# Chunks 16 and 17 of the input projection in three passes, the state norm inside the scan, two products on GpSimd

## The reference

```python
for l in range(DEPTH):                       # DEPTH = 2
    z = rmsnorm(x, norm_mix_g[l]) @ w_in[l]
    z_a, z_b, z_c, z_dz, z_dxbc, z_ddt, z_g = split_cols(z, IN_SPLITS)
    y_a = mixer_spatial_gating(z_a, ...)     # A
    y_b = mixer_pool(z_b, ...)               # B
    y_c = mixer_rwkv7(z_c, ...)              # C: decayed receptances r, keys k, state in 2 chunks of 128
    y_d = mixer_ssd(z_dz, z_dxbc, z_ddt, ...)   # D: ends in rmsnorm(y * silu(z_dz), d_norm_g)
    proj = einsum('btkc,kcd->btkd', stack([y_a, y_b, y_c, y_d]), w_branch[l])
    x = x + (sum(sigmoid(z_g) * proj) @ w_out[l])
    x = x + channel_mixer(rmsnorm(x, norm_ffn_g[l]))
return rmsnorm(x, norm_final_g)
```

## Time and profile before

| | us |
|---|---|
| median of 3 runs (lowest, highest) | 2014.98 (2013.32, 2015.97) |
| the profiled execution, its own time | 2014.89 |
| its span in the trace | 2013.1 |
| PE busy in the span | 1992.4 (99%) |
| PE weight loads | 1651.4 (82%) |
| DVE busy | 1518.5 (75%) |
| ACT busy | 1184.6 (59%) |
| POOL busy | 62.8 (3%) |
| granted TensorE clock, mean | 0.998 of full speed |

### The profile page before, as it was taken

The page is one execution under the profiler, slowest core; times in us unless marked ns, Lnnn a source line. Parts: engine busy times, 40 slices in busy tenths (PEclk is TensorE's granted clock), DMA queues, the critical chain, the costliest instruction groups (busy, mean ns, idle before and its releaser), DMA issues.

```text
span 2013.1 us, 31612 instructions
## 1 busy us (share of the span) xinstructions
PE 1992.4 (99%) x12922; PEld 1651.4 (82%) x12922; DVE 1518.5 (75%) x1498; ACT 1184.6 (59%) x1071; POOL 62.8 (3%) x56
## 2 busy tenths in 40 slices
PE   8999999999999999999999999999999999999998
PEld 8988899999999988999977777777777777777775
DVE  4888537766535779546688888888888888888887
ACT  4654445433334555444477776777767777677775
POOL 0200011000000020011000000000000000000000
PEclk9999999999999999999999999999999999999999
DMA  8523225555554523234469998999989999899994
GB/s 311 178 98 123 85 105 192 182 189 189 184 183 157 189 105 119 92 106 147 155 265 368 363 365 339 358 364 364 365 341 356 368 360 369 341 355 368 360 367 190
DMA packets 70792, 503.96 MB, mean 250 GB/s; under 512 B 8320, under 2 KB 8576, under 8 KB 9984
## 3 DMA queue, kind: packets, MB, share of 16 engines
q1 hardware_dynamic: 69792, 499.03, 66.1%
q10 hardware_dynamic: 864, 2.95, 0.4%
HBM read 500.90 MB, written 1.05 MB: 249 GB/s over the span
## 4 chain that ended last, share of the span: by engine, by line
PE 59%; DVE 2%; ACT 0%; issue 0%; DVEq 0%; ACTq 0%
PE g L536 38%; PE m L536 19%; PE m L1268 1%; DVE ring_low L2235 0%; PE m L831 0%; DVE arena L2145 0%; DVE h L2560 0%; PE m L586 0%; PE g L1030 0%; DVE rstd L2558 0%; DVE mg_low L2271 0%; PE m L1261 0%; DVE arena L2260 0%; DVE rep L2260 0%; DVE arena L2132 0%
## 5 line engine op out<-in xcount | busy, mean ns | idle before, releaser
L2295 DVE TENSOR_TENSOR ring_low<-ring,we_high 128x2048 fp32r<-128x2048 f32 x336 | 765.5, 2289 | 122.2 <-ACT we_high L1671 121.4
L1671 ACT ACTIVATE we_high<-ring 128x2048 fp32r<-128x2048 f32 x334 | 640.9, 1919 | 269.8 <-PE g L536 170.0
L536 PE MATMUL g<-h_high,ring_low 128*128 128x256 f32 x1328 | 372.2, 282 | 0.0
L536 PE MATMUL g<-we_high,hg_high 128*96 128x512 f32 x896 | 355.8, 397 | 0.0
L536 PE MATMUL g<-ring_low,hg_high 128*96 128x512 f32 x896 | 353.0, 394 | 0.0
L536 PE MATMUL g<-we_high,hg_low 128*96 128x512 f32 x896 | 352.0, 393 | 0.0
L536 PEld LDWEIGHTS g<-h_high,ring_low 128*128 128x128 f32 x1328 | 249.4, 189 | 0.0
L536 PE MATMUL g<-h_low,w_high 128*128 128x256 f32 x720 | 200.4, 282 | 0.0
L536 PE MATMUL g<-h_high,w_high 128*128 128x256 f32 x720 | 200.2, 281 | 0.0
L536 PEld LDWEIGHTS g<-we_high,hg_low 128*96 128x96 f32 x896 | 144.3, 161 | 63.3
L536 PEld LDWEIGHTS g<-we_high,hg_high 128*96 128x96 f32 x896 | 144.7, 161 | 58.8
(11 more groups left out here) (340 smaller groups left out, 3193.2 us busy)
## 6 DMA issues: line engine op xcount, KB each, us to landing
ring<-stream SPq DMA_DIRECT2D x472, 1024.0 KB, 4.8
sw<-sw_in SPq DMA_DIRECT2D x1, 1088.0 KB, 10.9
sw<-sw_in ACTq DMA_DIRECT2D x1, 1088.0 KB, 7.1
x<-x_in SPq DMA_DIRECT2D x4, 256.0 KB, 4.3
out<-h ACTq DMA_DIRECT2D x4, 256.0 KB, 2.8
cc<-cc_in SPq DMA_DIRECT2D x1, 816.5 KB, 12.2
rep<-rep_in SPq DMA_DIRECT2D x1, 768.0 KB, 13.5
rep<-rep_in ACTq DMA_DIRECT2D x1, 768.0 KB, 6.8
```

The lines of the kernel that those rows point to most:

```text
L536: return pe.matmul(o, a, b, start=start, stop=stop, skip_group_check=True)
L1671: A(we_high[n % 3][:, :], ring[:, slot, :], ACT.Copy).then_inc(high_ready, 1)
L2295: TT(ring_low[:, slot, :], ring[:, slot, :], we_high[n % 3][:, :], ALU.subtract).then_inc(low_ready, 1)
```

## The change

What is computed stays the same; two chunks are multiplied another way, and work moves between engines and places.

- Chunks 16 and 17 are multiplied in three passes, by two more `scan_high` on ACT and two more `scan_low` on DVE in each layer. A third buffer, `scan_third`, takes the rounded chunks 16 and 18; 17 goes into `scan_even`. The tile `kk` moves to make room, `st` too.
- PE does chunk 18 ahead of the head sums `ss`, and DVE subtracts chunk 18 ahead of `removal` (the scaled keys `kk`).
- DVE's two products for `ar[.., 1, :]` and `ka` go to POOL, which makes the first after ACT's two exponentials and the second after DVE's `k2`. PE waits for both (`ar_ready`) before it turns the keys.
- DVE's scaling of D's output by the norm moves from `mixer_d` into level 1 of half 0 of `mixer_c`; the reciprocal stays.
- `SIDE` gets two more quarters at `cg`, one more before the second pair of scores in each half, and one before `n` of half 1: 70 in all.

```diff
-SCAN_SPLIT = (14, 15, 18)
+SCAN_SPLIT = (14, 15, 16, 17, 18)
-SIDE = [("cg", 4), ("sr", 4), ("kt", 3)]
+SIDE = [("cg", 6), ("sr", 4), ("kt", 3)]
-    SIDE += [(f"s1{_c}", 1), (f"s2{_c}", 1), (f"s3{_c}", 1)]
+    SIDE += [(f"n{_c}", _c), (f"s0{_c}", 1), (f"s1{_c}", 1), (f"s2{_c}", 1), (f"s3{_c}", 1)]
...
+        scan_third = part("scan_third", 23144, [CW])
...
-            return (scan_even if n % 2 == 0 else scan_odd)[:, :]
+            return {14: scan_even, 15: scan_odd, 16: scan_third, 17: scan_even, 18: scan_third}[n][:, :]
...
+                pe.wait_ge(S["ar_ready"], 2 * (l + 1))
                 pe.wait_ge(S["ab_ready"], l + 1)
                 turn(l, "kt", [ka[:, j, 0:P] for j in range(4)])
...
                 mixer_b(l)
+                project(l, 18, NZ)
                 pe.wait_ge(S["krsq"], l + 1)
                 pe.wait_ge(S["by_head_ready"], 1)
                 head_sums(l, "ss", tmp1)
-                project(l, 18, NZ)
...
                 q.step(A(small[:, 63:64], eps, ACT.Exp))
+                act.wait_ge(S["pooled"], l + 1)
+                scan_high(l, 16)
                 act.wait_ge(S["d_endraw"], l + 1)
...
                 drain(l, "st", A(st[:, :, :], mb("st")[:, :].rearrange("p (g n) -> p g n", g=2), ACT.Copy))
+                scan_high(l, 17)
...
+                pool.wait_ge(S["e_ready"], 4 * l + 2)
+                for i in range(2):
+                    g_done(pool, l, ("c", i))
+                G.tensor_tensor(ar[:, :, :, 1, :], zc[:, 0:4, 1:T + 1].rearrange("p j (c t) -> p j c t", c=NCH),
+                                e_in.rearrange("p j (c t) -> p j c t", c=NCH), ALU.mult).then_inc(S["ar_ready"], 1)
+                pool.wait_ge(S["k2_ready"], l + 1)
+                G.tensor_tensor(ka[:, :, :], k2[:, :, :], e_neg[:, :, :], ALU.mult).then_inc(S["ar_ready"], 1)
...
+                    if i == 1:
+                        scan_low(l, 16)
...
                         decay_sum(l)
+                        scan_low(l, 17)
                         mix(l, 4)
...
                 decay_mid(l)
-                removal(l)
                 mixer_a_out(l)
                 scan_low(l, 18)
+                removal(l)
                 mix(l, 5)
...
-                q.add(TT(ar[:, :, :, 1, :], rc, e_in.rearrange("p j (c t) -> p j c t", c=NCH), ALU.mult), v_seq)
-                q.step(TT(ka[:, :, :], k2[:, :, :], e_neg[:, :, :], ALU.mult))
                 q.step(TT(nb[:, :, :], aa[:, :, :], e_neg[:, :, :], ALU.mult), S["ab_ready"])
+                dve.wait_ge(S["ar_ready"], 2 * (l + 1))
...
+                        if (c, lv) == (0, 1):
+                            mixer_d_norm(l)
```

More of the change, by code:

```diff
@@ L265, in trunk @@
         cs = tiles(21648, H, P)
-        st = tiles(22672, 2, T)
+        st = tiles(12840, 2, T)
         seg1 = tiles(25192, H, P)
@@ L290, in trunk @@
         kept = small[:, 128:128 + L * CT].rearrange("p (l j) -> p l j", l=L)
-        w_log, c_sum, aa, kk = (tiles(at, 4) for at in (26216, 27240, 9744, 23144))
+        w_log, c_sum, aa, kk = (tiles(at, 4) for at in (26216, 27240, 9744, 15976))
         e_in, e_neg, e_ex = (tiles(at, 4) for at in (7696, 8720, 22120))
@@ L787, in mixer_c @@
                     half = lambda hd: slice(64 * (hd % 2), 64 * (hd % 2) + 64)
+                    side(f"n{c}")
                     for q in range(2):
@@ L809, in mixer_c @@
                                     fill(l, st_, last)
-                        if p:
-                            side(f"s{p}{c}")
+                        side(f"s{p}{c}")
                     for v in range(LEVELS - 1):
@@ L1515, in mixer_c @@
                 for c in range(NCH):
-                    side(f"s1{c}", f"s3{c}")
+                    side(f"n{c}", f"s3{c}")
                     for v in range(LEVELS):
@@ L1568, in z_highs @@
                     if n < N_SLOTS:
-                        act.wait_ge(chunks_used, chunk0(l) + NZ - (1 if (2 * l * N_LATE + n) % N_SLOTS < 3 else 0))
+                        act.wait_ge(chunks_used, chunk0(l) + NZ - 1)
                     A(half_slot(l, m, b), half_ring(ring, l, m, b), ACT.Copy).then_inc(z_high_ready, 1)
@@ L2006, in mixer_d, with mixer_d_norm @@
                 m_done(dve, l, "dn")
-                q.step(V.reciprocal(rstd[:, :], rms[:, :]))
+                q.step(V.reciprocal(rms[:, :], rms[:, :]))
+            def mixer_d_norm(l):
                 for j in range(4):
-                    ins = V.scalar_tensor_tensor(yD[:, j, :], yD[:, j, :], par(l, "norm_d", j), rstd[:, :], ALU.mult, ALU.mult)
+                    ins = V.scalar_tensor_tensor(yD[:, j, :], yD[:, j, :], par(l, "norm_d", j), rms[:, :], ALU.mult, ALU.mult)
                     (q.add(ins, v_seq) if j == 0 else q.add(ins, S["yd_ready"]))
@@ L2050, in keys @@
                 for j in range(4):
-                    q.add(V.scalar_tensor_tensor(k2[:, j, :], k2[:, j, :], 1.0, zc[:, 4 + j, 1:T + 1], ALU.add, ALU.mult), v_seq)
+                    ins = V.scalar_tensor_tensor(k2[:, j, :], k2[:, j, :], 1.0, zc[:, 4 + j, 1:T + 1], ALU.add, ALU.mult)
+                    (q.add(ins, v_seq) if j < 3 else q.step(ins, S["k2_ready"]))
                 dve.wait_ge(v_seq, q.n[id(v_seq)])
@@ L2164, in mixer_c @@
                             drain(f"t{lv}{c}", V.tensor_copy(tt[64:P, :, 0:64], mb(f"t{lv}{c}")[64:P, :].rearrange("p (i t) -> p i t", i=H)))
+                        if (c, lv) == (0, 1):
+                            mixer_d_norm(l)
+                        if (c, lv) == (1, 5):
+                            y_lows(l, 3)
                         if (c, lv) == (0, 5):
```

7 lines of the change are left out of this document (2 added, 5 removed).

## The result

The changed kernel takes **2037.43 us** (median of 4 runs, 2034.48 to 2038.69) beside 2014.84 of the kernel before (2013.32 to 2015.97); the ratio is **1.0111**, 95% interval 1.0093 to 1.0128. That is 22.6 us slower. The direction was forecast, the size (+5.6, at most +11) was not. The profiled execution of the changed kernel is its fastest, 2034.48 us; the other three (2036.29 to 2038.69) show a mean granted clock of 0.992 where this one has 0.994.

The account below looks back on a forecast made before the run. PE was taken as the bound, with DVE and ACT close behind. Terms of +2.0, -2.3, +2.6 and +0.45 made +2.8 us per layer, +5.6 on 2014.89: 2020.5 us, likeliest case 2016.0 to 2023.0, 8-in-10 range 2007.0 to 2026.0.

Parts of the forecast that it names:

- The passes: Scan: chunks 16 and 17 in three passes instead of four save PE 2.4 us per layer.
- The hold: Before chunk 18: POOL's first product blocks DVE's product or subtraction for 2.1 us, so PE waits 2.7.
- balance: First quarter after chunk 18: net of the forecast's gains and waits up to there, +2.3 us per layer.
- the turned keys: Stretch from the first quarter to `n`: balance +2.0 us per layer, with keys ready before PE wants them.
- term 6: `mixer_c`: added quarters cover PE's waits of 0.78, 0.7 and 0.53, and the 0.30 goes too; -2.3 us per layer.
- A: Rival, chance 0.22: DVE and POOL hardly hold each other up; -1.0 us per layer, 2012.9 us.
- B: Rival, chance 0.20: ACT's and DVE's chain to the first half chunk is shorter than its rows; -5.2 per layer, 2004.5 us.
- C: Rival, chance 0.08: POOL's strided product takes 4.10 us, each of two meetings costs DVE 2.0 more; 6.6 per layer, 2028.1 us.
- Term 7: `mixer_c`: moved half chunks and gate products delay PE, +0.45 us in half 0 and +2.6 before `x` in half 1.
- term 4: Before the first quarter: ACT's later chain and POOL's hold delay the first half chunk, so PE waits 2.0 us.
- Term 5's last sentence: Before `n`: taking two products off DVE ends no PE wait, keys being ready before the projection quarters are done.
- the first terms: Scan to first quarter: passes, ACT's and DVE's added work, POOL's hold and ACT's chain; together +2.3 us per layer.

Follow-up runs that it names:

- b3: Changed kernel with the half chunks early as in a3, and ACT's gate of half 1 behind its two copies for level 0; ratio 1.0022.
- a1: Changed kernel with useless products put into two of PE's waits, ahead of chunk 18 and of level 0 of half 1; ratio 1.0070.
- a4: Changed kernel with the old table of side quarters except at `cg`, which keeps six; ratio 1.0037.
- d1: Kernel before with only the changed table of side quarters, and the last branch's low parts a level earlier; ratio 1.0092.
- a2: Changed kernel with the two products back on DVE, ahead of the last removal product; ratio 1.0120.
- a3: Changed kernel with two half chunks of each half subtracted between the scores instead of behind the last ones; ratio 1.0054.
- b2: Changed kernel in which POOL starts its first product only when chunk 18's low part is there; ratio 1.0119.
- c3: Kernel before with only the two products moved from DVE to POOL; ratio 1.0048.
- c1: Changed kernel with half chunks, ACT's gate and low parts reordered, ACT and DVE work moved into their waits, POOL's first product behind the first removal; 2007.4 us, ratio 0.9952.
- d2: c1 with the two products back on DVE at their old place, the seventh half chunk ahead of them; 2007.3 us, ratio 0.9947.

## Why the prediction was wrong

**Right.** The passes (-2.4 per layer; 1.24 for one chunk). The hold: DVE's product lost 1.98 us, forecast 2.1, and PE waited 2.01 before chunk 18, forecast 2.7. The first quarter stood 2.9 us later than before, of which 1.2 is the start of the run: balance +1.7, forecast +2.3. At the turned keys (176.38 for 170.95, less two quarters of 1.43 and the start's 1.2) it was +1.4, forecast +2.0. The four waits of `mixer_c` went, as term 6 said. Rivals A and B are refuted by the 2.67 and by b3's 1.49, C by POOL's 2.17. C's time of 2028.1 came nearest by number only (by its own terms, 2.8 and twice 2.0, it would be 6.8 per layer and 2028.5).

**Two steps failed.** Term 7 and what belongs to it had the waits in `mixer_c` 4.4 us per layer too low, 8.8 in all; and there was no clock in the sum, net 5.4 us. Either alone takes the time out of the range that ended at 2026: as an estimate, 2037.4 less 8.8 is 2028.6, less 5.4 it is 2032.0.

**No clock.** I added up waits as if each cost its length. Five low stretches cost 8.5 us more than the one of before. The one at chunk 18 stood mostly in the place of the wait that term 4 had forecast before the first quarter (a1, a4, b3), so net 0.1 to 0.2 each; those in half 1, 1.7 each, and the longer one at the merge's end, 1.7 more than before, came on top. In the trace of before the clock was 1.00 wherever the change was made, so no row there tied a fall to a wait; but the row at 994 showed that it could fall.

**Term 7, half 0: 0 to +0.7 forecast, 2.51 measured.** The instructions were counted right (five half chunks in a row), but only against `t`. The quarter behind the last scores now needed the first of them. That PE's own order had moved ahead of DVE's was to be read from the order of the two engines, without any trace; d1 shows the wait in the kernel before with nothing else changed. The 1.13 at the second branch's low parts, forecast at nothing, was missed in the same way.

**Term 7, half 1: 2.6 forecast, 0.89 + 2.16 measured, by another way.** I made DVE's masked product late; in fact ACT's copies were late behind its gate, which waits for POOL, which waits for DVE (b3). The size agreed by chance.

**Term 5's last sentence** was wrong under the new table (a2), without effect on the sum. Per layer, from start to start of PE's rows and from the forecast +2.8: -0.6 at the first terms, +2.1 and +1.4 (the second branch) in half 0, +0.9 of waits and +1.7 of clock in half 1, gives 8.3; with 0.5 for three quarters that take 1.6 instead of 1.43 it is 8.8, where 8.4 was measured, so the rows add up to within 0.4. Over both layers the 8.4, with the start (1.2) and the merge's end (1.7), is the 19.6 of the span. The 3 us between that and the 22.6 of the medians lie outside the profiled executions; their mean clock, 0.992 for 0.994, would make up to 4, as an estimate.

**Open** is what decides whether a wait is followed by a fall. The changed kernel, a3, a4 and b3 do the same up to chunk 18 and wait 2.0 us there; in their eight layers the clock fell five times, and in a4 in one layer and not in the other. The wait behind the scores of half 0 has a fall in a2, b2 and d1 but none in the changed kernel. Nor does length alone decide: of 36 waits of 2.0 to 2.75 us in the mixers of all profiled runs 28 had one, and so had both of 1.22 us in a4. Open too are the low stretches around the end of the merge, which cost 1.7 to 8.5 us with no wait ahead of them; they blur a single execution by up to 0.0034, and the medians by less.

## What to carry to other kernels

A wait of the engine that bounds the kernel may cost more than its length, because its clock can fall behind it; look at the granted clock of the stretch after each wait, and don't read "busy" as "at speed". When a quarter of work is moved forward on one engine, check on each other engine what produces its input and behind what that stands; a wait between two short operations is where such a producer fits. Giving work to POOL can cost DVE more than the work did: here 3.4 us of holds for 2.4 of products, and earlier (c3). Started in DVE's own waits it did no harm, but gained nothing either (c1 beside d2). Don't take parts that add up as proof that the parts are all there.

## What the runs showed of the hardware

- After 28 of 36 PE waits of 2.0 to 2.75 us the granted clock was at its lower level (0.50) for 3.4 us, which costs 1.7 us of work, and after the other 8 it stayed at 1.00. Behind a wait of 1.22 us (a4) it fell too. Products of no use in the waits kept it up (a1, four of four).
- It also fell with no wait ahead, near the end of the merge, for 3.4 to 10.4 us (1.7 to 5.1 us of work).
- A low clock is counted as busy time: 28 products in 3.00 busy us at one level, 16 at the other.
- POOL's product of 1024 elements took 2.17 to 2.50 us when DVE did not hold it, and held DVE's operations with two tiles of SBUF (2.67 for 0.69, 4.55 for 2.36) and with one (3.09 for 1.14). When DVE was first by 0.04 us, POOL's took 3.42.
